# Seven experts in blocks of 64 places, gathers over 128 partitions and w_down in rows of 8 KB

## The reference, cut to what matters

```python
logits = tok @ router_w + router_b                      # 512 x 32
top_vals, top_idx = lax.top_k(logits, TOP_K)            # 4 experts for each token
gate_w = jax.nn.softmax(top_vals, axis=-1)
# for each expert, its tokens x (on average 64 of them):
g, u = split(x @ w_up[e] + b_up[e])                     # w_up[e] 1024 x 2048, 8 MB
g = jnp.minimum(g, 7.0); u = jnp.clip(u, -7.0, 7.0)
act = (u + 1.0) * (g * jax.nn.sigmoid(1.702 * g))
out = act @ w_down[e] + b_down[e]                       # w_down[e] 1024 x 1024, 4 MB
y[token] += gate_w * out
```

## Time and profile before

| what | value |
|---|---|
| median of three runs | 2009.8 us |
| the profiled execution | 2009.08 us, span 2007.3 us |
| PE busy | 1957.2 us (98%) |
| DVE, ACT, POOL busy | 35%, 24%, 5% |
| PE matmul `psum<-arena` at L1927 | 11360 records, 1121.4 us |
| DMA | 511.75 MB, mean 255 GB/s over the span |
| GB/s of a fortieth of the span, from 900 us to 1900 us | 385 to 408 |
| granted PE clock, mean | 0.994 |

### The profile page before, as it was taken

One profiled execution on the slowest core, in us unless ns is written; L12 is line 12 of the kernel. 1 busy time (PEld: TensorE's weight loads), 2 busy tenths in 40 slices (PEclk: granted clock), 3 DMA queues, 4 the chain that ended last, 5 costly groups with the idle time before them and its releaser, 6 DMA issues.

```text
span 2007.3 us, 38970 instructions
## 1 busy us (share of the span) xinstructions
PE 1957.2 (98%) x16190; PEld 1165.7 (58%) x16190; DVE 709.8 (35%) x1085; ACT 490.5 (24%) x742; POOL 99.0 (5%) x130
## 2 busy tenths in 40 slices
PE   6999999999999999989999999999999999999998
PEld 4777878888888888624444444444444444444447
DVE  5667778778764443521010101010101010101056
ACT  3444352543524332200101010101010101010135
POOL 2000000001010000000000000000000000000020
PEclk9999999999999999989999999999999999999999
DMA  4222232222222543489999999999999999999962
GB/s 130 73 69 79 54 83 74 63 63 63 64 65 82 153 124 123 198 342 386 402 396 399 398 399 399 396 400 398 400 396 401 385 406 388 407 388 405 400 230 117
DMA packets 204508, 511.75 MB, mean 255 GB/s; under 512 B 14165, under 2 KB 126054, under 8 KB 171686
## 3 DMA queue, kind: packets, MB, share of 16 engines
q1 hardware_dynamic: 189296, 474.68, 63.0%
q0 software_dynamic: 5888, 20.97, 3.5%
q10 hardware_dynamic: 9270, 15.35, 2.1%
HBM read 493.59 MB, written 17.37 MB: 255 GB/s over the span
## 4 chain that ended last, share of the span: by engine, by line
PE 93%; DVE 4%; ACT 2%; issue 1%; ACTq 0%; DMA 0%; DVEq 0%; POOLq 0%
PE psum L1927 89%; PE psum L2318 1%; PE psum L2326 1%; DVE arena L1389 1%; PE psum L1989 0%; PE psum L2097 0%; ACT w_hi L793 0%; PE psum L2057 0%; PE psum L2042 0%; DVE w_lo L1273 0%; DMA arena<-h_dram,slot_token 0%; DVE arena L1457 0%; DVE arena L1303 0%; DVE arena L1368 0%; DVE residual L1856 0%
## 5 line engine op out<-in xcount | busy, mean ns | idle before, releaser
L1927 PE MATMUL psum<-arena 128*32 128x512 f32 (+4 forms) x11360 | 1121.4, 522 | 10.6 <-DVE arena L1389 5.3
L1927 PEld LDWEIGHTS psum<-arena 128*32 128x32 f32 (+2 forms) x11360 | 481.9, 115 | 606.0 <-issue 464.8
L1792 DVE TENSOR_SCALAR arena<-psum 128x768 f32<-128x768 f32 x32 | 30.6, 957 | 965.5 <-ACT arena L1110 965.5
L1927 PE MATMUL psum<-h_hi,w_hi 128*128 128x512 f32 x640 | 258.6, 404 | 1.3 <-DVE w_lo L1273 1.3
L1927 PE MATMUL psum<-h_hi,w_lo 128*128 128x512 f32 x640 | 249.8, 390 | 0.0
L1927 PE MATMUL psum<-h_lo,w_hi 128*128 128x512 f32 x640 | 249.4, 390 | 0.0
L1273 DVE TENSOR_TENSOR w_lo<-arena,w_hi 128x1024 fp32r<-128x1024 f32 x104 | 135.7, 1305 | 187.6 <-ACT w_hi L793 186.6
L1110 ACT ACTIVATE arena<-psum 128x768 f32<-128x768 f32 x32 | 26.0, 811 | 595.8 <-PE psum L1927 595.8
L1927 PEld LDWEIGHTS psum<-h_hi,w_hi 128*128 128x128 f32 x640 | 120.3, 188 | 34.3 <-issue 8.7
L1927 PEld LDWEIGHTS psum<-h_lo,w_hi 128*128 128x128 f32 x640 | 120.4, 188 | 26.3 <-issue 2.9
L1927 PEld LDWEIGHTS psum<-h_hi,w_lo 128*128 128x128 f32 x640 | 120.1, 188 | 25.8
(11 more groups left out here) (356 smaller groups left out, 1635.6 us busy)
## 6 DMA issues: line engine op xcount, KB each, us to landing
arena<-in_w_up SPq DMA_DIRECT2D x256, 1024.0 KB, 13.6
arena<-in_w_down SPq DMA_DIRECT2D x128, 1024.0 KB, 14.6
arena<-in_w_in SPq DMA_DIRECT2D x80, 512.0 KB, 3.9
y_dram<-arena ACTq DMA_DIRECT2D x31, 288.0 KB, 6.2
arena<-in_w_ssd_branch SPq DMA_DIRECT2D x16, 512.0 KB, 3.8
arena<-in_w_attn_branch SPq DMA_DIRECT2D x8, 512.0 KB, 3.7
arena<-in_w_out SPq DMA_DIRECT2D x8, 512.0 KB, 4.3
pg_raw<-in_w_ple_gate SPq DMA_DIRECT2D x8, 512.0 KB, 12.8
```

Of the source, the lines that this page charges most:

```text
L1792: dve.tensor_scalar(u_sb, up_psum[:, :, 1, :], 1.0 + LIMIT, 1.0 - LIMIT, ALU.min, ALU.max).then_inc(u_ready, 1)
L1927: return pe.matmul(o, l, r, start=start, stop=stop)
```

## The change

- Of experts 2 to 30, the seven with the fewest tokens run at positions 3, 7, ..., 27 with 64 places; the other 22 keep 96 and fill the other positions, and experts 0, 1 and 31 keep theirs. DVE sorts them in a chain of `max` operations and writes the order to `control`; SP, POOL and ACT read it there each round. `tables_ready` has three steps now, and `rows_u` is written last. If the seventh has more than 64 tokens, the flag is set and 28 more rounds run.
- A small expert uses `up_small`, `down_small`, 4 transposes for 6, smaller copies and a store of 64 rows.
- PE, ACT and DVE run loops of seven trips with four rounds in each (`GROUP`), POOL and SP loops of one round.
- `fetch` gathers 128 rows. Places 96 to 127 have the token 0 (`slot_token` is cleared first).
- Partition p of a `w_down` pair holds rows 2p and 2p + 1, and `turn_act` takes every second column of `hidden` to match.
- The rows 64 to 95 of all blocks of `y_dram` are zeroed by 8 stores of 0.5 MB on ACT's queue during attention, and rows 0 to 63 of the last block as before.

```diff
+GROUP, SMALLS, FIRST_SMALL, PAIR = 4, 7, 3, 64
+AGAIN = EXTRA + SMALLS
+ROUNDS = EXPERTS + AGAIN
+FLAG = ROUNDS + AGAIN
...
-        w_dn_d = w_down[0].rearrange("e (c a p) n -> e c p a n", p=P, a=2)
+        w_dn_d = w_down[0].rearrange("e (c p a) n -> e c p a n", p=P, a=2)
...
+            sp.wait_ge(tables_ready, 3)
...
             with sp.Fori(2, EXPERTS) as i:
-                load_up(i, i)
-                load_bias_up(i, i)
-                load_down(i - 1, i - 1)
-                load_bias_down(i - 1, i - 1)
+                e = owner_of(i)
+                load_up(i, e)
+                load_bias_up(i, e)
+                e = owner_of(i - 1)
+                load_down(i - 1, e)
+                load_bias_down(i - 1, e)
...
+            pool.memset(slot_token[:], 0)
...
-                    pool.tensor_copy(block_token[0:CAP, :], slot_token[0:CAP, ds(b, 1)]).then_inc(block_token_ready, 1)
+                    if column is None:
+                        column = pool.value_load(control[0:1, ds(b, 1)], min_val=0, max_val=BLOCKS - 1)
+                    pool.tensor_copy(block_token[:], slot_token[:, ds(column, 1)]).then_inc(block_token_ready, 1)
...
-                pool.indirect_dma_start(xg[0:CAP], None, h2_dram, bass.IndirectOffsetOnAxis(token, 0)
+                pool.indirect_dma_start(xg, None, h2_dram, bass.IndirectOffsetOnAxis(token, 0)
...
+            def zero_third_strips(h):
+                act.dma_start(third_strips[:, ds(h * 4, 4), :], zero_rows[0:STRIP].unsqueeze(1).broadcast_to([STRIP, 4, D])
+                              ).then_inc(y_zeroed, 16)
...
+                at_block = act.value_load(control[0:1, ds(b + (AGAIN if kept else 0), 1)], min_val=0, max_val=BLOCKS - 1)
...
+            own.then(dve.max(smallest[0:1], key[0]))
+            own.then(dve.scalar_tensor_tensor(out=owner[0:1, 31:32], in0=smallest[0:1, SMALLS - 1:SMALLS],
+                                              scalar=-float(EXPERTS * P * PAIR + P), in1=inc[0:1, EXPERTS - 1:EXPERTS],
+                                              op0=ALU.is_lt, op1=ALU.add))
+            dve.tensor_copy(control[:, FLAG:FLAG + 1], owner[0:1, 31:32]).then_inc(tables_ready, 1)
...
+                for k in range(4 if small else 2 * STRIPS):
+                    ins = pe.transpose(turned_act[:, k, :], hidden[:, k // 2 * QUARTER + k % 2:(k // 2 + 1) * QUARTER:2], ident[:])
...
+            def up_small(b):
...
+                    for r in range(2):
+                        for c in (r, 2 + r):
+                            for j in range(2):
+                                ins = mm(bank(r)[strip(c - r + j)], x_T[:, k, strip(j)],
+                                         up_both[k][:, :, c * QUARTER:(c + 1) * QUARTER], k == 0, False)
...
+            def down_small(i):
...
+                    for half in range(2):
+                        for j in range(2):
+                            ins = mm(bank(4)[strip(2 * half + j)], act_T[:, 2 * (c % 2) + k % 2, strip(2 * (c // 2) + j)],
+                                     w[:, half * 512:half * 512 + 512], k == 0, False)
...
-            def round_of(b):
-                up(b)
+            def round_of(b, small=False, small_behind=False):
+                (up_small if small else up)(b)
                 turn_x(b + 1, b)
-                down(b - 1)
-                turn_act(b)
+                (down_small if small_behind else down)(b - 1)
+                turn_act(b, small=small)
...
+                with pe.Fori(2, 2 + GROUP * SMALLS, GROUP) as b:
+                    for c in range(GROUP):
+                        round_of(b + c, small=c == 1, small_behind=c == 2)
+                round_of(EXPERTS - 2)
```

More of the change, by code:

```diff
@@ L732, in _ @@
                 pool.wait_ge(h2_stored[b], 16 * TT // 2)
-            experts(0, EXPERTS)
+            fetch(0)
+            fetch(1)
+            pool.wait_ge(tables_ready, 3)
+            with pool.Fori(2, EXPERTS) as b:
+                fetch(b)
             def gather_rows(rows):
@@ L1155, in _ @@
             swish(1)
-            rounds(2, EXPERTS - 1, 0)
+            with act.Fori(2, 2 + GROUP * SMALLS, GROUP) as b:
+                for c in range(GROUP):
+                    copy_act(b + c - 1, small=c == 2)
+                    expert_out(b + c - 2, small=c == 3)
+                    swish(b + c, small=c == 1)
+            copy_act(EXPERTS - 3)
+            expert_out(EXPERTS - 4)
+            swish(EXPERTS - 2)
             copy_act(EXPERTS - 2)
@@ new lines, in _ @@
+            dve.tensor_copy(control[:, FLAG:FLAG + 1], owner[0:1, 31:32]).then_inc(tables_ready, 1)
+            own.mark(dve.max_index(small_at[0:1], smallest[0:1], key[0]))
+            own.then(dve.scalar_tensor_tensor(out=key[1], in0=key[0], scalar=smallest[0:1, SMALLS - 1:SMALLS],
+                                              in1=iota_far[0:1, sorted_of], op0=ALU.is_lt, op1=ALU.mult))
+            own.mark(dve.tensor_copy(small_of[0:1], small_at[0:1]))
+            own.then(dve.max(others[0:1, 0:8], key[1]))
@@ L2319, in turn_x, with turn_act @@
                 ins.then_inc(x_turned, 1)
-            def turn_act(i, last=False):
+            def turn_act(i, last=False, small=False):
                 pe.wait_ge(act_ready, i + 1)
@@ new lines, in experts @@
+            def experts():
+                turn_x(0, 0)
+                up(0)
+                turn_x(1, 0)
+                turn_last_slots()
+                turn_act(0)
+                round_of(1)
+                with pe.Fori(2, 2 + GROUP * SMALLS, GROUP) as b:
+                    for c in range(GROUP):
+                        round_of(b + c, small=c == 1, small_behind=c == 2)
+                round_of(EXPERTS - 2)
+                up(EXPERTS - 1)
+                down(EXPERTS - 2)
+                turn_act(EXPERTS - 1, last=True)
+                down_last(EXPERTS - 1)
@@ L2424, in experts, with experts_again @@
+            def experts_again():
+                turn_x(EXPERTS, EXPERTS)
+                up(EXPERTS)
+                turn_x(EXPERTS + 1, EXPERTS)
+                turn_act(EXPERTS)
+                with pe.Fori(EXPERTS + 1, ROUNDS - 1) as b:
                     round_of(b)
-                up(end - 1)
-                down(end - 2)
-                turn_act(end - 1, last=True)
-                (down if first else down_last)(end - 1)
+                up(ROUNDS - 1)
+                down(ROUNDS - 2)
+                turn_act(ROUNDS - 1, last=True)
+                down(ROUNDS - 1)
```

238 lines of the change are left out of this document (150 added, 88 removed).

## The result

| | before | after |
|---|---|---|
| median | 2009.9 us | 1994.0 us (1991.96 to 1994.8) |
| span of the profiled execution | 2007.3 us | 1990.2 us |
| TensorE busy | 1957.2 us | 1901.5 us |

The ratio is 0.9917, with a 95% interval of 0.9900 to 0.9934: the change wins 16 us, where 47 were forecast. The direction and the range hold; the size does not.

The account below looks back on a forecast made before the run. PE bounds the kernel before, with the DMA almost a second bound; after the change the DMA sets the end. Its gain of 51.3 less 4 at the end is 47 us: 2009.8 - 47 is 1962 us, range 1938 to 2001.

Parts of the forecast that it names:

- the turn of the loop: PE's branch back in the expert loop: 3.37 us, leaving 2.4 us idle a turn, 14.4 us at six turns.
- Rival 1: PE's loop turns cost more, each also halving the clock for some 10 us: gain 31, 1978 us; chance 0.15.
- rival 3: PE stays the bound, as the DMA is sped up more or code is held: 1934 to 1948 us; chance 0.12.
- The small rounds: PE's rounds of small experts: shorter `up`, `down` and `turn_act` save 10.8 us each, seven times 75.6 us.
- the strided transposes: PE's transposes reading every second column of `hidden`: 0 to 0.8 us a round, taken as 0.
- PE's side: PE's time for rounds 2 to 29: 939.1 less 75.6 plus 14.4 is 877.9 us, a gain of 61.2.
- The DMA's side: DMA work in the expert loop: 34.11 falls to 32.54 us a round, 887.8 us in all, a gain of 51.3.
- the 0.31 us of the longer rows: Loads of `w_down` in rows of 8 KB instead of 4 KB: 0.31 us less DMA work a round.
- rival 2: The DMA dip at gathers does not come from 96 partitions and stays or grows: 2009 to 2017 us; chance 0.22.
- The ceiling on a landing: A part of `w_up` in the expert loop may take 30.9 us from issue to landing.
- The 4 us for a late `w_ple_gate`: At the kernel's end, the last 2 MB of `w_ple_gate` come late: 4 us on the path.
- Costed at nothing: DVE's table chain, added register loads and stores of zeros in attention (0 to 2.6 us, taken as 0): no cost.

Follow-up runs that it names:

- written-out kernel: The kernel after, with PE's 28 rounds of the loop written out one behind the other, so no branch back: 1974.9 us.
- experiment 10: The kernel after, with the two full rounds of a group made an inner loop of two trips, so three bodies for four: 1990.3 us.
- the loop alone: The kernel before, with only PE's loop changed to seven trips of four large rounds, the last round behind it: 2061.2 us.
- the path first: PE's code for no full expert put ahead of the other: 1986.0 us in the kernel after, 1967.0 us with the rounds written out.
- experiment 4: The kernel before, with only w_down's rows 2p and 2p + 1 on partition p and the strided transposes they need: 2014.5 us.
- experiment 3: The kernel before, with only the gathers over 128 partitions, 32 more rows, all of them token 0: 2010.7 us.
- the loops of two and three rounds: The kernel before, with PE's loop of one round made a loop of two or of three rounds: 2009.9 us and 2076.5 us.

## Why the prediction was wrong in size

**The step that failed is the turn of the loop.** "I take the upper" put a turn at the 3.37 us of the only code miss in the trace, less 0.8 hidden, and no clock. I called that an upper bound; it was one sample, of a jump ahead. Measured: a branch of 6.1 us, a gap of 5.2, and the clock behind it. By GpSimd's periods over a turn, on average 41.3 us for the 33.6 of the written-out kernel, that is 7.7 us a turn and 46 us for six, in place of 14.4. The sample had been taken where the DMA share was 0.04, and all turns stand where it is about 1. Rival 1 had the right kind of loss, with the same stretch as its evidence, but started from the gap of 2.4 us, so it stopped at 1978 us and got 0.15. Of rival 3 the condition came true, that PE stays the bound, but with the cost of rival 1 on top.

**The start was not a step of mine at all.** The jump was in the kernel before as well, and I costed nothing there because nothing about it was changed. The edits moved where its target lies in the code; in the kernel after that brought the second stop, 5.7 us, and in that of experiment 10 there is none.

**The small rounds** were close. A group of four takes 124.17 us in the written-out kernel before the DMA binds, 134.15 before the change: 9.98 us, 69.9 for seven, against 75.6. Of the missing 5.7, the strided transposes, costed at 0 within 0 to 0.8 us a round, are 28 x 0.11 = 3; the rest I have not located.

PE's side then is 69.9 - 46 - 5.7 = 18 us, and the profiled spans differ by 17.1. The experiments are of the same size: the loop alone costs 50.3 us, the path first wins 8.

**The DMA's side** came out right as a sum, 32.54 us forecast and 32.57 measured where it binds, and that was luck. With the gather of 96 rows the written-out kernel takes 33.5 us a round, where the forecast's other terms give 34.11 - 0.31 - 0.08 + 0.19 = 33.9; and the gather is worth 0.9 us and not 1.37. The two errors of some 0.45 us cancel. Where the first lies stays open: in the 34.11 us, which were read from landings beside a dip that is no constant, or in a small term. Of these, the 0.31 us of the longer rows did not show in experiment 4. That the dip comes with the gather over 96 partitions is shown (experiment 3), and rival 2 is out. The ceiling on a landing was taken as 30.9 us and is 26.7: 4.2 us less to spare. With the late start that makes 10 of the 13 us by which the written-out kernel misses 1962. The 4 us for a late `w_ple_gate` were half of that at most: from the last gather of the loop to the end takes 156.9 us there for 154.9 before.

That the later side sets the end was the right frame. I had the sides 10 us apart (gains of 61.2 and 51.3), and the one with the less certain term came out 43 lower.

**Costed at nothing**: the table chain, the register loads and the stores of zeros show no new wait on PE, and the first gather stands at 852.4 us before and after; these held.

The Trainium skill, Runtime: NRT & Kernel Launch, section Instruction fetch mechanics, has PE hold 2048 instructions, and says that a taken branch whose target is not in the current window of two pages stalls on a fetch. By the 2048 the six stalls were certain, and the loops of two and three rounds (some 1,500 and 2,250 records of PE) agree with it. The body of experiment 10, some 1,950 records, does not: it should be held and is not. And two pages, which are 32 KiB there, would not hold even the one round of the kernel before, which turned in 208 ns. The section has no price, and the price was what decided.

## What to carry to other kernels

Before you unroll a hardware loop, work out the body's code in bytes: with some 94 KB a turn of PE cost 0.2 us here, with some 125 KB and more 8 us, gap and clock together. A price from a single row is a sample and not a bound; when a term is multiplied by the trips of a loop, a loop of nothing else changed measures it in one run. Check that a run that is to take a load away takes it away where you look. And put the path that is always taken first: the jump over the other one still costs some 4 us at the end, but here 9 us left the start, 5.5 of them a second stop that depends on where the target lies.

## What the runs showed that I had not expected

- A turn back to code that PE does not hold takes 5.6 to 6.4 us beside a DMA share of about 1. The jump ahead to such code takes 3.3 to 3.8 us at shares under 0.7, and 4.4 to 4.8 us in the three cases with 0.8 to 1.0.
- Behind each of the six gaps of 5.2 us PE's granted clock was 0.50 (1.2 GHz) for a while; behind the gap of 2.5 us in the earlier trace rows it stayed at 1.00.
- A gather over 96 partitions beside transfers over 128 draws the stream from 423 GB/s to between 280 and 340; the same gather over 128 left it at 415 to 420 in the rows above.
- A transpose of 128 x 128 in fp32 that reads its weights at every second column takes 300 ns on average, for 282.
